# Moving the activation tile H and the coefficient ring by 128 and 256 bytes in a two-block transformer kernel

## The chip, the cores and the metric

The kernel runs on one core of one Trainium2 chip. The metric is the device time of one execution in microseconds (us). A core has five engines with a program each: TensorE (PE, matrix products), VectorE (DVE), ScalarE (ACT), GpSimd (POOL) and SyncE (SP, which here only issues transfers). They share an on-chip memory of 128 partitions, and each tile named below is a range of bytes that is the same in all partitions.

## The reference

Two transformer blocks run one after the other over 256 tokens of width 1024, in float32. What matters of it:

```
# first block
hn = modulate(rmsnorm(x, norm1_g), shift1, scale1);  proj = hn @ w_in
ya = dsa_attention(...);  yb = stick_breaking_attention(...)
x  = x + gate1 * ((sigmoid(ga)*(ya @ w_proj_a) + sigmoid(gb)*(yb @ w_proj_b)) @ w_out)
hn2 = modulate(rmsnorm(x, norm2_g), shift2, scale2)
# expert layer: 16384 experts, 8 heads, 16 experts for each head and token
pre  = einsum('cd,chkd->chk', hn2, u[experts]);  coef = gates * gelu(pre)
x  = x + gate2 * einsum('chk,chkd->cd', coef, v[experts])
# second block
x = x + hybrid_mixer(rmsnorm(x));  x = x + memory_cross_attention(rmsnorm(x), rmsnorm(mem))
h = rmsnorm(x);  u = causal_dwconv(h @ w_up);  x = x + (silu(a) * g) @ w_down
```

The output is a last rmsnorm of x, (1, 256, 1024).

## The kernel before, in words

**Weights as a stream.** All weights come from main memory in units of 128 x 1024 float32 (512 KB). Each unit is split into two float32r parts whose sum is the weight: ACT copies the upper part (line 1298), and DVE (line 1834) or POOL (line 2625) subtracts it from the weight to get the rest. The parts lie in a ring of buffers, `split` (three buffers, lines 377 and 484), with further ones in `split1`, `split4` and `split5` in some phases. Activations are held split in the same way.

**Products.** A product of two split numbers takes three matmuls (`mm3`, line 613, all recorded at line 611): upper x upper, upper x rest, rest x upper. In most layers (`lin`, line 655) the weight is the stationary operand, 128 x 128, and the activations of all 256 tokens are the moving operand, 128 x 256: in the profile `bank<-H,split ... 128x256`. One unit is 24 such matmuls. `bank` is the accumulation memory that TensorE writes.

**The tile H.** `H_all` (line 381) has 16 + 16*256 float32 in each partition. Two views lie in it. `H` (line 382) holds the normed activations, z = 0 the upper parts of eight 128-channel blocks k, z = 1 the rests: each (z, k) is 256 floats, 1024 bytes. It is the moving operand of the input projections, the output projection w_o, the routing projection w_pq, all of `u` and, in the second block, the mixer's and feed-forward's first layer. `Hf` (line 472) is the same memory, 16 floats further on, cut into eight pairs `cf[i]` of 512 floats (line 473): the ring of coefficients of the expert layer's second half.

**The expert layer.** In the u phase PE multiplies all 16384 rows of u with H (128 units, `lin("u", ...)`, line 1023). From unit 56 on, 12 small bf16 matmuls stand between units (`spread_gates`, line 1000), which spread the chosen gates over the experts; their operands lie in turn in `rT` and in the two halves of `xT`. In the v phase (lines 1030 to 1040) the coefficients `cf[i]` are stationary and a v unit is moving, 128 x 512: `bank<-split,H ... 128x512`, 12 a unit. ACT writes the upper part of `cf[i]` (line 1637) and DVE the rest (line 2373), four units ahead.

**The hand-over.** The first coefficients are written over parts of H that PE still reads for the last u unit. So in that unit PE counts up the semaphore `h_past` after k = 2, 4 and 6 (line 693), and ACT waits for it before cf[0], cf[1] and cf[2] (line 1642); cf[3] waits for the end of the unit. cf[0] covers floats 16 to 527 of the tile, and so H's upper parts k = 0, 1 and the first 16 floats of k = 2.

**Where tiles lie.** Tiles get addresses in the order in which they are asked for. Ahead of H stand `ringb` (16384 bytes a partition), `split` (24576), `xT` (8192) and `mod` (48 floats, 192 bytes); behind it `cst`, `vecs`, `sm`, `cond`, `rT`. From `split`'s first byte, `H` begins 24576 + 8192 + 192 = 32960 bytes on, which is 128*256 + 192 (64 bytes short of a multiple of 256), and `Hf` 33024 bytes on, which is 129*256. The tiles `Ya`, `Yb`, `Ym`, `MH` and `act_t`, moving operands as H is, begin 64 bytes short of a multiple of 256 from `split` too, some of them by tiles `gap0` to `gap4` of 64 bytes that hold nothing, and all weight buffers begin at a multiple of 256 bytes from each other.

Of the kernel before, what the change touches and what calls it, by code (L numbers as in the profile page):

```python
# [16 lines left out]
T = 256  # L17
# [56 lines left out]
def flat(ap):  # L74
    return ap.rearrange("p a b -> p (a b)")
# [244 lines left out]
def scaled_before(q):  # L320

    return q - (q > 4)
# [38 lines left out]
def build(nc, A, out, scratch, x_kept):  # L361
    with ExitStack() as ctx:
# [6 lines left out]
        def sb(name, shape, dt=F32, where=ctx):  # L369
            return where.enter_context(nc.sbuf_tensor(name, shape, dt))  # L370
# [5 lines left out]
        ringb = sb("ringb", [128, 4, UNIT])  # L376
        split = sb("split", [128, 3, 2, UNIT], F32R)
        xT = sb("xT", [128, 8, T])
        mod = sb("mod", [128, 48])

        H_all = sb("H", [128, 16 + 16 * T], F32R)
        H = H_all[:, 0:16 * T].rearrange("p (z k t) -> p z k t", z=2, k=8)
        cst = sb("cst", [128, 768])
        vecs = sb("vecs", [128, A["vecs"].shape[1]])
        sm = sb("sm", [128, 160])
        cond = sb("cond", [128, 8])
        rT = sb("rT", [128, 5, T])
# [81 lines left out]
        iota2 = rt[:, 2, 0:128].bitcast(BF16).rearrange("p (i b) -> p i b", b=2)  # L469
        g2 = PR[:, 80 * 256:80 * 256 + 256].rearrange("p (t n) -> p t n", t=2)  # L470
        cpf = PR[:, 81 * 256:81 * 256 + 512].rearrange("p (t z n) -> p t z n", t=2, z=2)
        Hf = H_all[:, 16:16 + 16 * T]
        cf = [(Hf[:, i * 512:i * 512 + 256], Hf[:, i * 512 + 256:i * 512 + 512]) for i in range(8)]

        xkT, xv, bmm, mqT, mkT, mv, ccT, uT, ctmp, gqk, goT, gv, lrT, sc_b, gt = pieces(
# [74 lines left out]
        def evac(name, p):  # L550

            eng, n = EV[name, p]
            return (ev_a if eng == "A" else ev_v, n)
# [13 lines left out]
        def unscaled(q):  # L567

            return (Ym, H, MH)[q - 3], 8 * (q - 3)

# [34 lines left out]
        def tensor_program(t):  # L605
# [7 lines left out]
            def mm3(o, l, r, start, stop):  # L613
                mm(o, l[0], r[0], start, False)
                mm(o, l[0], r[1], False, False)
                return mm(o, l[1], r[0], False, stop)

            def claim(b):
                if freed[b]:
                    t.wait_ge(*freed[b])  # L620
                return banks[b]
# [20 lines left out]
            def unit(name, conc=3):  # L642
                while U[st["pos"]][0] == "w_ada":
                    ada_unit()
                n = st["pos"]
                assert U[n][0] == name, (U[n], name)
                st["pos"] += 1
                jobs.step(conc)
                if P.lo_pool[n]:
                    t.wait_ge(lo_g, P.lo_no[n])  # L650
                else:
                    t.wait_ge(lo_v, P.lo_no[n])
                return buf(n)

            def lin(name, ncols, rhs, need, kt=8, conc=3, after_block=None, after_unit=None, both=False, order=range(8), alone=0, begin=0):
                left = n = 0
                for p in range(begin, ncols // 2):
                    b = None
                    if both and p == begin:


                        b = bank_of[name, p]
                        two = {}
                        steps = [(k, j) for j in range(2) for k in order[:alone]] + [(k, j) for k in order[alone:] for j in range(2)]
                        for k, j in steps:
                            if j not in two:
                                two[j] = unit(name, conc)
                                claim(b)
                            need(k)
                            wh, wl = two[j]  # L670
                            last = mm3(banks[b][:, j * T:(j + 1) * T], (wh[:, k * 128:(k + 1) * 128], wl[:, k * 128:(k + 1) * 128]), rhs(k),
                                       k == order[0] and j == 0, k == order[-1])
                            if k == order[-1]:
                                last.then_inc(pe_done, 1)
                        freed[b] = evac(name, p) if name != "w_up" else (f_t2, 2 * p + 2)
                        if after_block:
                            after_block(p)
                        continue
                    for j in range(2):
                        for k in range(kt):  # L680
                            if left == 0:
                                wh, wl = unit(name, conc)
                                left = 8
                            if b is None:
                                b = bank_of[name, p]
                                claim(b)
                            o = (8 - left) * 128
                            left -= 1
                            need(k)
                            last = mm3(banks[b][:, j * T:(j + 1) * T], (wh[:, o:o + 128], wl[:, o:o + 128]), rhs(k), k == 0, k == kt - 1)  # L690
                            if left == 0 or (j == 1 and k == kt - 1):
                                last.then_inc(pe_done, 1)
                            elif name == "u" and n == 127 and k in (2, 4, 6):

                                last.then_inc(h_past, 1)
                            if left == 0 and after_unit:
                                after_unit(n)
                                n += 1
                    freed[b] = (f_t2, 2 * p + 2) if name == "w_up" else evac("gated" if ("gated", p) in EV and name == "u" else name, p)
                    if after_block:  # L700
                        after_block(p)
# [28 lines left out]
            def of(X):  # L730
                return lambda k: (X[:, 0, k, :], X[:, 1, k, :])

            def of_t(X):
                return lambda k, tt: (X[:, 0, k, tt * 128:(tt + 1) * 128], X[:, 1, k, tt * 128:(tt + 1) * 128])

            hk, hkt = of(H), of_t(H)

# [130 lines left out]

            mh = normed(0)
            lin("w_qi", 4, hk, mh, both=True)  # L870
            one("w_ki", hk, mh)

# [27 lines left out]

            jobs.start(index_steps())
            lin("w_qb", 4, hk, mh)
            lin("w_kb", 4, hk, mh)
            lin_nat("w_vb", hkt, mh, 512)

# [379 lines left out]
        def scalar_program(s):  # L1285
# [68 lines left out]
            def squares(q, name):  # L1354
                def later(c):
                    for i in (2 * c, 2 * c + 1):
                        s.wait_ge(ev_v, EV[name, c][1] - 1 + i % 2)
                        if q in (3, 4):
                            high(q, i)
                    for i in (2 * c, 2 * c + 1):  # L1360
                        square(q, i, xT[:, i, :])
                    yield
                return lambda c: jobs.start(later(c))
# [16 lines left out]
            def hi_of(i):  # L1380
                return MH[:, 0, :, :] if i == 2 else H[:, 0, :, :]

# [171 lines left out]
            for c in range(4):  # L1554
                unit("w_pa")
                s.wait_ge(mg_sum, c + 1)
                S.copy(flat(H[:, 0, 2 * c:2 * c + 2, :]), sg[:, c * 512:(c + 1) * 512]).then_inc(mg_hi, 1)
            add = squares(1, "w_o")
# [265 lines left out]
        def vector_program(v):  # L1824
# [90 lines left out]
            def norm_steps(i, src, gain, shift=None):  # L1915
                for j in range(8 if shift is None else 10):
# [5 lines left out]
                    if shift is not None and j >= 2:  # L1922
                        v.wait_ge(n_hi, 8 * scaled_before(i) + j - 1)
                        V.scalar_tensor_tensor(out=H[:, 1, j - 2, :], in0=rT[:, ROW[(j - 2) % 4], :], scalar=shift(j - 2),
                                               in1=H[:, 0, j - 2, :].bitcast(F32), op0=ALU.add, op1=ALU.subtract).then_inc(n_lo, 1)
# [1016 lines left out]
```

## Time and profile before

| | |
|---|---|
| three runs | 1439.8, 1435.71, 1439.47 us; median 1439.47 |
| profiled execution | 1439.8 us; its span, first to last instruction, 1438.1 us |
| mean granted TensorE clock | 0.988 of full speed |
| PE busy | 1390.4 us, 97% of the span |
| DVE, ACT, POOL busy | 1095.1, 836.4, 359.6 us |
| matmuls | 10406 in the records |

The profile's records give the start and duration of each instruction. A matmul's duration holds its way through the array, and successive matmuls overlap: how fast they follow each other is read from a stretch's length over its count, not from the duration. Some matmul records are missing.

### The profile page before, as it was taken

How to read it: one execution, taken by the hardware profiler on the slowest of the kernel's cores; microseconds unless marked ns; L12 is line 12 of the kernel's file. 1: busy time of each engine (PE TensorE's matmuls, PEld its weight loads, DVE VectorE, ACT ScalarE, POOL GpSimd, SP SyncE). 2: the span in 40 equal slices, each digit the busy share in tenths (PEclk: the TensorE clock that was granted, in tenths of full speed). 3: DMA queues.
4: the chain of work that ended last, by engine and by line, in shares of the span. 5: the costliest groups of instructions: out<-in, count | busy, mean ns of one | idle time of the engine just before them, and what ended most of it. 6: DMA issues, size and time to landing. Idle time of an engine off the chain costs nothing.

```text
span 1438.1 us, 25879 instructions
## 1 busy us (share of the span) xinstructions
PE 1390.4 (97%) x10406; PEld 1292.4 (90%) x10406; DVE 1095.1 (76%) x1903; ACT 836.4 (58%) x1447; POOL 359.6 (25%) x227
## 2 busy tenths in 40 slices
PE   7999999899999999999999999999999999899997
PEld 5988899899999999999988888887889899799997
DVE  7788897567889888999766666677667667798862
ACT  4554774444454687777654454565446666776651
POOL 3216201234445100000032322344322321433200
PEclk9999999999999999999999999999999999999999
DMA  9768775556665454444566666665667636276630
GB/s 387 273 200 266 250 247 170 164 156 184 189 185 161 153 156 148 147 148 147 151 189 221 195 192 195 212 198 178 197 191 254 195 115 193 75 248 191 196 113 30
DMA packets 73721, 268.24 MB, mean 187 GB/s; under 512 B 8401, under 2 KB 9730, under 8 KB 72834
## 3 DMA queue, kind: packets, MB, share of 16 engines
q1 hardware_dynamic: 71280, 256.41, 56.1%
q10 hardware_dynamic: 1426, 7.56, 1.5%
q0 software_dynamic: 896, 2.62, 0.5%
q8 instruction: 83, 1.36, 0.4%
q14 instruction: 36, 0.29, 0.1%
HBM read 262.88 MB, written 3.67 MB: 185 GB/s over the span
## 4 chain that ended last, share of the span: by engine, by line
PE 80%; DVE 13%; ACT 4%; POOL 1%; DMA 1%; issue 1%; DVEq 0%; ACTq 0%; POOLq 0%
PE bank L611 79%; DVE split L1834 3%; DVE ada_acc L1869 2%; DVE PR L2284 1%; DVE PR L2281 1%; DMA ringb<-in_w_ada 1%; POOL H L2652 1%; ACT split L1298 1%; DVE PR L2289 1%; PE bank L787 0%; DVE rT L1920 0%; POOL split L2625 0%; DVE H L2373 0%; DMA vecs<-in_vecs 0%; DVE PA L2085 0%
## 5 line engine op out<-in xcount | busy, mean ns | idle before, releaser
L611 PE MATMUL bank<-H,split 128*128 128x256 f32 x5928 | 724.8, 283 | 17.9 <-DVE split L1834 6.8
L611 PEld LDWEIGHTS bank<-H,split 128*128 128x128 f32 x5928 | 703.1, 191 | 24.7 <-issue 9.4
L1298 ACT CAST split<-ringb 128x1024 fp32r<-128x1024 f32 x350 | 365.9, 1047 | 284.8 <-PE bank L611 270.4
L2625 POOL TENSOR_TENSOR split<-ringb,split 128x1024 fp32r<-128x1024 f32 x91 | 226.7, 2491 | 665.6 <-ACT split L1298 665.6
L611 PE MATMUL bank<-split,H 128*128 128x512 f32 (+1 forms) x1728 | 390.5, 387 | 1.5 <-POOL split L2625 1.5
L1834 DVE TENSOR_TENSOR split<-ringb,split 128x1024 fp32r<-128x1024 f32 x259 | 326.0, 1262 | 74.9 <-ACT split L1298 74.8
L611 PEld LDWEIGHTS bank<-split,H 128*128 128x128 f32 x1728 | 320.9, 188 | 69.1 <-POOL split L2625 2.5
L2373 DVE TENSOR_TENSOR H<-PR,H 128x256 fp32r<-128x256 f32 x128 | 137.3, 1073 | 106.4 <-ACT H L1637 106.4
L1298 ACT CAST split<-far 128x1024 fp32r<-128x1024 f32 x89 | 93.1, 1048 | 53.4 <-PE bank L611 43.1
L1834 DVE TENSOR_TENSOR split<-far,split 128x1024 fp32r<-128x1024 f32 x77 | 99.7, 1304 | 31.5 <-ACT split L1298 31.3
L1613 ACT ACTIVATE PR<-bank 128x512 f32<-128x512 f32 (+31 forms) x59 | 28.7, 487 | 74.5 <-PE bank L611 74.5
L2639 POOL TENSOR_TENSOR rT<-rT 128x256 f32<-128x256 f32 x25 | 26.7, 1067 | 176.4 <-ACT rT L1347 174.8
L611 PE MATMUL bank<-act_t,split 128*128 128x256 f32 x528 | 60.3, 276 | 0.8 <-DVE act_t L2594 0.8
L611 PEld LDWEIGHTS bank<-act_t,split 128*128 128x128 f32 x528 | 60.0, 188 | 1.0 <-DVE act_t L2594 1.0
L1596 ACT ACTIVATE xT<-cst,rT 128x128 bf16<-128x128 f32 x168 | 55.6, 437 | 0.0
L1637 ACT CAST H<-PR 128x256 fp32r<-128x256 f32 x128 | 51.1, 400 | 0.6 <-PE bank L611 0.6
L2346 DVE TENSOR_TENSOR PR<-bank,PR 128x224 f32<-128x224 f32 (+31 forms) x64 | 33.2, 519 | 21.7 <-PE bank L611 21.1
L2336 DVE TENSOR_TENSOR xT<-rt,cpw 128x512 bf16<-128x512 bf16 x126 | 45.7, 417 | 0.0
L2625 POOL TENSOR_TENSOR split<-far,split 128x1024 fp32r<-128x1024 f32 x12 | 30.4, 2530 | 54.6 <-ACT split L1298 54.6
L611 PE MATMUL bank<-Ym,split 128*128 128x256 f32 x336 | 41.7, 283 | 1.5 <-DVE Ym L1995 1.5
L611 PEld LDWEIGHTS bank<-Ym,split 128*128 128x128 f32 x336 | 40.2, 189 | 2.3 <-DVE split L1834 1.7
L611 PE MATMUL bank<-xT 128*128 128x128 bf16 x504 | 36.2, 219 | 0.0
(298 smaller groups left out, 1264.4 us busy)
## 6 DMA issues: line engine op xcount, KB each, us to landing
ringb<-in_u SPq DMA_DIRECT2D x128, 512.0 KB, 3.8
ringb<-in_v SPq DMA_DIRECT2D x128, 512.0 KB, 4.4
ringb<-in_w_ada SPq DMA_DIRECT2D x28, 512.0 KB, 5.4
far<-in_w_up SPq DMA_DIRECT2D x26, 512.0 KB, 4.3
far<-in_w_ada SPq DMA_DIRECT2D x20, 512.0 KB, 5.2
ringb<-in_w_up SPq DMA_DIRECT2D x17, 512.0 KB, 4.7
ringb<-in_w_pq SPq DMA_DIRECT2D x16, 512.0 KB, 4.2
far<-in_w_dn SPq DMA_DIRECT2D x14, 512.0 KB, 4.2
```

What stands on the lines that cost most here:

```text
L611: return TE.matmul(o, l, r, start=start, stop=stop, skip_group_check=True)
L1298: S.copy(buf(m)[0], slots[P.slot[m]]).then_inc(hi_done, 1)
L1596: S.activation(z[:, i // 2, :, i % 2], iota, ACT.Abs, bias=cpn[:, 4 * g + i:4 * g + i + 1]).then_inc(t_abs, 1)
L1613: ins = S.activation(d[:, :, n:T], o[:, :, n:T], ACT.Gelu)
L1637: S.copy(cf[i % 8][0], P3[:, i, :]).then_inc(c_hi, 1)
L1834: V.tensor_tensor(lo, slots[P.slot[m]], hi.bitcast(F32), ALU.subtract).then_inc(lo_v, 1)
L1869: V.scalar_tensor_tensor(out=acc, in0=w, scalar=cond[:, k:k + 1], in1=acc, op0=ALU.mult, op1=ALU.add).then_inc(ada_done, 1)
L2336: ins = V.tensor_tensor(t_gate[g % 3][:, z, :, :, :], t_col[g % 2], of_four(gp[:, 2 + z, :], g), ALU.mult)
L2346: V.tensor_tensor(d[:, 0:n, :], o[:, 0:n, :], d[:, 0:n, :], ALU.mult).then_inc(t_out, 1)
L2373: V.tensor_tensor(lo, P3[:, i, :], hi.bitcast(F32), ALU.subtract).then_inc(c_lo, 1)
L2625: G.tensor_tensor(lo, slots[P.slot[m]], hi.bitcast(F32), ALU.subtract).then_inc(lo_g, 1)
L2639: G.tensor_tensor(acc, acc if k > 1 else rT[:, square_row(q, 0), :], rT[:, square_row(q, k), :], ALU.add).then_inc(sq_add, 1)
```

## The change

The first edit places `mod` behind `vecs` instead of ahead of H; so H_all, cst and vecs begin 192 bytes lower. The second lets `H` begin at float 16 of H_all (it was float 0) and `Hf` at float 0 (it was float 16). With both, `H` lies 128 bytes lower than before and `Hf` 256 bytes lower. From `split`'s first byte `H` is then at 32832 = 128*256 + 64, and `Hf` at 32768 = 128*256. cst and vecs lie 192 bytes lower, mod behind them; no other tile moves. The third edit fits the hand-over to this: cf[0] now covers floats 0 to 511 and so k = 0 and the larger part of k = 1, and PE counts after k = 1, 3 and 5. On all five engines the same instructions stand in the same order as before.

```diff
         xT = sb("xT", [128, 8, T])
-        mod = sb("mod", [128, 48])
 
         H_all = sb("H", [128, 16 + 16 * T], F32R)
-        H = H_all[:, 0:16 * T].rearrange("p (z k t) -> p z k t", z=2, k=8)
+        H = H_all[:, 16:16 + 16 * T].rearrange("p (z k t) -> p z k t", z=2, k=8)
         cst = sb("cst", [128, 768])
         vecs = sb("vecs", [128, A["vecs"].shape[1]])
+        mod = sb("mod", [128, 48])
         sm = sb("sm", [128, 160])
...
-        Hf = H_all[:, 16:16 + 16 * T]
+        Hf = H_all[:, 0:16 * T]
         cf = [(Hf[:, i * 512:i * 512 + 256], Hf[:, i * 512 + 256:i * 512 + 512]) for i in range(8)]
...
-                            elif name == "u" and n == 127 and k in (2, 4, 6):
+                            elif name == "u" and n == 127 and k in (1, 3, 5):
 
                                 last.then_inc(h_past, 1)
```

## Rows read from the trace of the kernel before

**Rows 1.** The page, part 1: busy time, share of the span, instructions.
```profile
PE 1390.4 (97%) x10406; PEld 1292.4 (90%) x10406; DVE 1095.1 (76%) x1903; ACT 836.4 (58%) x1447; POOL 359.6 (25%) x227
```

**Rows 2.** The chain that ended last: start us, us, what.
```profile
35.86 17.20 PE bank L611 x144
...
315.72 102.91 PE bank L611 x872
...
483.60 249.97 PE bank L611 x2493
...
736.74 238.27 PE bank L611 x1050
...
1257.23 109.11 PE bank L611 x936
```

**Rows 3.** The page, part 5: line, operation, count | busy, mean ns | idle before.
```profile
L611 PE MATMUL bank<-H,split 128*128 128x256 f32 x5928 | 724.8, 283 | 17.9 <-DVE split L1834 6.8
```

**Rows 4.** Windows, all engines: us, busy by engine (count), clock, DMA share, GB/s.
```profile
316.00:419.00 103.00, 103.00 (x877) 103.00 (x876) 84.09 (x292) 50.89 (x59) 42.86 (x18) 1.00 0.61 183
487.00:733.00 246.00, 246.00 (x2460) 243.42 (x2458) 211.95 (x434) 179.15 (x404) 7.19 (x3) 1.00 0.51 153
```

**Rows 5.** Windows, PE alone, matmuls that read or write tile H.
```profile
320.00:400.00 80.00, 80.00 (x682) 1.00 0.61 185
1280.00:1340.00 60.00, 60.00 (x532) 1.00 0.62 195
...
750.00:900.00 150.00, 150.00 (x663) 1.00 0.65 201
1119.00:1126.00 7.00, 7.00 (x32) 1.00 0.82 237
```

**Rows 6.** Tile H on PE, 320 to 400 us: duration min/median/max.
```profile
L611 PE MATMUL bank<-H,split x682: 281/281/281, 319.7 to 400.0; 128*128 128x256 f32 x171
```

**Rows 7.** Tile H on PE, 1280 to 1340 us.
```profile
L611 PE MATMUL bank<-H,split x532: 276/276/276, 1279.8 to 1340.0; 128*128 128x256 f32 x178
```

**Rows 8.** Timeline of PE in the u phase: start us, us, operation, count.
```profile
583.05 3.07 PE L611 MATMUL bank<-H,split 128*128 128x256 f32 x24
585.96 0.86 PE L611 MATMUL bank<-xT 128*128 128x128 bf16 x12
...
590.21 2.99 PE L611 MATMUL bank<-H,split 128*128 128x256 f32 x24
593.04 0.86 PE L611 MATMUL bank<-rT 128*128 128x128 bf16 x12
```

**Rows 9.** Timeline of PE in the w_pq projection, key scores between.
```profile
273.15 5.91 PE L611 MATMUL bank<-H,split 128*128 128x256 f32 x48
278.90 1.05 PE L611 MATMUL bank<-PR 128*128 128x128 f32 x8
279.71 5.71 PE L611 MATMUL bank<-H,split 128*128 128x256 f32 x48
285.25 0.94 PE L611 MATMUL bank<-PR 128*128 128x128 f32 x7
```

**Rows 10.** Tiles Yb and act_t on PE, whole span: duration min/median/max.
```profile
L611 PE MATMUL bank<-Yb,split x96: 276/281/387, 201.9 to 215.1; 128*128 128x256 f32 x96
...
L611 PE MATMUL bank<-act_t,split x528: 276/276/386, 1366.2 to 1427.0; 128*128 128x256 f32 x176
```

**Rows 11.** Matmuls with cst, by line and form.
```profile
L611 PE MATMUL bank<-rT,cst 128*128 128x256 f32 x46 | 14.2, 454 | 1.9 <-ACT rT L1347 1.9
```

**Rows 12.** Timeline of all engines at the hand-over from u to v.
```profile
733.59 0.76 ACT L1637 CAST H<-PR 128x256 fp32r<-128x256 f32 x2 [0.30 <-PE bank L611]
...
733.74 4.43 PE L611 MATMUL bank<-split,H 128*128 128x512 f32 x17
...
734.25 0.58 ACT L1615 ACTIVATE bank<-bank 128x512 f32<-128x512 f32 x1
...
735.48 1.21 DVE L1834 TENSOR_TENSOR split<-ringb,split 128x1024 fp32r<-128x1024 f32 x1
...
736.74 1.23 PEld L611 LDWEIGHTS bank<-split,H 128*128 128x128 f32 x6 [0.49 <-DVE split L1834]
```

## The prediction

> **What bounds the kernel now.** I read the page's busy times first: PE is busy for 1390.4 of 1438.1 us [rows 1]. The chain of waits, in order of time, then says where PE itself sets the end [rows 2]: five long pieces without a wait in them, 17.20 us at 36, 102.91 at 316, 249.97 at 484, 238.27 at 737 and 109.11 at 1257, together 717 us. In the two pieces that matter most the other engines have room: from 316 to 419 us DVE is busy for 84.09 of 103 us, ACT for 50.89, and the DMA engines for 0.61 of the time; from 487 to 733 us it is 211.95 and 179.15 of 246, and 0.51 [rows 4]. PE is without a gap in both. What shortens PE's matmuls there shortens the kernel by as much; what lengthens them does the same.
>
> The instructions and their order do not change, so the question is whether an address changes the speed of an instruction. The reader should look at the same instruction at two places: a 128x256 matmul with H moving and a weight of `split` stationary. From 320 to 400 us 682 records fill 80.00 us, from 1280 to 1340 us 532 fill 60.00 [rows 5]. Taking off the two that only hang over an edge, one starts every 80.00/680 = 117.6 ns in the first and every 60.00/530 = 113.2 ns in the second. The granted clock is 1.00 in both windows, so this is not the clock. The durations say the same without an edge: 281/281/281 ns against 276/276/276 [rows 6, 7]. There are two settled rates, and the difference is 4.4 ns a matmul, nearly 4%. I call them slow and fast.
>
> Over the whole span the mean with H is 283 ns for 5928 matmuls [rows 3], with some at the slower clock in it; by the stretches counted below about 2,900 of them, half, are slow. What selects a rate? Within a stretch it is constant over all k, upper and rest, and over all buffers of the ring: 872 matmuls in 102.91 us from 316 us on, 118.0 ns each, all slow [rows 2]. It changes only where other matmuls stand between. In the w_pq projection, 48 matmuls from 273.15 to the key scores at 278.90 take 5.75 us and the next 48, from 279.71 to 285.25, take 5.54 us [rows 9]; this alternation goes on for eight groups. In the u phase the unit from 583.05 to 585.96 takes 2.91 us, that from 590.21 to 593.04 2.83 us [rows 8], and the pattern slow, slow, fast repeats over the 64 gate groups. Other moving tiles, which lie 64 bytes short of a multiple of 256 bytes from `split` as H does, show both too: Yb has 276 as its smallest and 281 as its median, act_t 276 as its median over 528 [rows 10]. So at this distance both rates are stable once entered. That looks like two streams of reads, moving operand and next weights, that get in each other's way or not, depending on how they stand to each other. Where they stand is what an address distance sets.
>
> **The change, part by part.**
>
> *H against split, from 64 bytes below a multiple of 256 to 64 above.* Nothing in the trace has a 256-wide matmul at the new distance with the weight stationary, so I bound the cost from both sides by the two rates that exist. All H stretches fast, where PE sets the end:
> - 36 to 53 us, 144 slow: 144 x 4.4 ns = 0.64 us.
> - w_pq, four slow groups of 48: 4 x (5.75 - 5.54) = 0.84 us.
> - 316 to 419 us, 872 slow: 3.84 us.
> - u phase: of 64 units with gates 43 slow at 2.91 - 2.83 = 0.08 us, 3.44 us, and eight units after the last gates (711 to 733 us, 186 matmuls) at 24 x 4.4 ns, 0.84 us.
> - the rest (slow parts of the attention projections, the routing stretch 419 to 483 us where DVE sets the pace half of the time, and the second block's short layers): an estimate from some 450 slow matmuls, 2.0 us, of which half counts, 1.0 us.
>
> The sum is 0.64 + 0.84 + 3.84 + 4.28 + 1.0 = 10.6 us of gain. Nothing takes it back as long as DVE has the 19 and 34 us of room of [rows 4]; in the u phase a fast unit already exists every third time without PE waiting.
>
> All H stretches slow: the feed-forward's 936 matmuls from 1257 us on [rows 2] lose 4.1 us, 21 fast u units 1.7, w_pq 0.8, the 165 behind the first piece 0.7, and the other fast ones, some 1100 in the attention and mixer layers, 4.8 us of which 3.7 count since other engines set the pace in part. That is 11.0 us of loss. So this term is between -10.6 and +11.0 us. I take -10.6: half of the matmuls are slow at the old distance, which is therefore no good one, and the other half shows that nothing in the instruction stream forbids the fast rate. It is a choice, not a derivation.
>
> *Coefficients, Hf, 256 bytes lower.* Its distance to `split` stays a multiple of 256. In the v phase 663 records fill 150.00 us [rows 5], 150.00/661 = 226.9 ns, twice the fast rate. The nearest other row has H itself as the stationary operand with a 512-wide moving one, at a distance of 64 bytes: 7.00 us for 32 records [rows 5], or about 30.5 matmuls, 229 ns. So the price of a bad place is 2.3 ns x 1536 = 3.5 us, and there is none better in the trace. I take 0, because the distance modulo 256 is kept, and keep 0 to +3.5 for the range.
>
> *H as the stationary operand* in the value projections: 192 matmuls, 144 of them 512 wide, at most 2.3 ns each, below 0.5 us either way. I take 0.
>
> *cst 192 bytes lower.* It is the ones or identity operand. The largest group is 46 matmuls, 14.2 us [rows 11]; with 4% on these and the few like them, 0.6 us on either side. I take 0. mod and vecs are read by vector instructions of a few hundred nanoseconds, for which no row hints at an effect of the address.
>
> *Hand-over one k earlier.* In the last u unit PE counts `h_past` one group of three matmuls earlier, 0.35 us. PE goes from its last u matmul to its first v matmul without a gap at 733.74 [rows 12], so nothing is won there. The one wait of PE is 0.49 us at 736.74 for the rest part of the second v unit, which DVE starts at 735.48. Queued ahead of it on DVE is the product that waits for ACT's Gelu at 734.25, which needs the end of the u phase. ACT's third and fourth casts are at 733.59; the third can go 0.35 us earlier, the fourth waits for the last u matmul as before, so the Gelu moves by less than 0.1 us. Worth 0 to -0.1 us; I take 0.
>
> **Sum.** -10.6 us on the profiled execution: its span 1438.1 becomes 1427.5, its time 1439.8 becomes 1429.2. The median of the runs, 1439.47, lies 0.3 us below that execution; so 1428.9 us, rounded to 1429.
>
> **A rule against it.** The rows above show one instruction at two rates at one clock, and the 4.4 ns between them. The Trainium skill says otherwise on both counts. "SBUF — State Buffer", section "Who interferes with whom", gives TensorE one read port for the moving operand and an independent one for the weights, and states that "PE and ACT never wait on anyone"; "TensorE: Matmul & The Clock Gate", section "Wait — 56ns, not 53.3ns?", gives the warm start-to-start as N / 2.4 GHz plus about 2.5 ns, 109.2 ns for N = 256, with no word of an address. By these the change would do nothing and the time would be 1439.5 us. The trace does not agree with them in size, 113.2 and 117.6 ns; whether the address is what they miss, no row shows.
>
> **The rivals.**
>
> *No net effect.* The rate may be picked by how TensorE comes out of the small matmuls and waits between units, which the change leaves as they are; or both rates stay stable at the new distance and the stretches are dealt anew. For it: both rates occur at one and the same distance, and groups of 48 alternate while their addresses repeat. Against it: in the value projections and the v phase two distances give 229 and 226.9 ns for one shape [rows 5], with no 226.9 in the one and no 229 in the other. If nothing changes, 1439.5 us. If they are dealt anew in the same proportion, the two long blocks, 3.8 us at 316 and 4.1 us at 1257, may go either way: 1435 to 1443.
>
> *The slow rate everywhere.* At the new distance each matmul with H meets the weight reads. The place is the feed-forward's first layer at 1257 to 1366 us, now wholly fast, then 117.6 instead of 113.2 ns. For it: all tiles of the kernel's fastest stretches (act_t, H in the feed-forward) have the old distance and none the new; where H was stationary and the distance was 64 bytes the other way, the 512-wide rate was the worse. Against it: the old distance is slow half of the time as well. It decides from the point at which more than half of the H matmuls are slow; in full, +11.0 us, 1450.5 us.
>
> *The coefficients pay.* H gets fast but the v phase gets the 229 ns: 1429 + 3.5 = 1432.5; with H unchanged, 1443.
>
> **How the numbers follow.** Forecast (H mostly fast) 0.42, own range 1426 to 1434. No net effect 0.27. Slow rate 0.27. Coefficients or something outside the two rates 0.04. What a measurement of this kernel can tell from no change is about 0.3%, 4.3 us. Faster holds the forecast, a part of the deal-anew case and half of the last, 0.45; slower the slow case and a part of the deal-anew case, 0.30; within 0.3% the remaining 0.25. The range goes from 1425 to 1451: the lower end is the full gain with some of the mixed stretches counted whole, the upper end the full loss.
>
> **What would show it.** Right: in the window 320 to 400 us the median duration with H is 276 ns and the count rises to about 708; the chain's piece of 872 matmuls takes 99 us; all u units between gates take 2.83 us; the v phase keeps 226.9 ns; act_t and Yb keep theirs. Wrong: a median of 281 in the feed-forward, or the same alternation as in [rows 8, 9] at the same places (then the address has no part), or a third rate, which would be outside my bounds.

## The result, and the profile after

The changed kernel takes 1447.41 us, the median of 10 runs (1441.86 to 1453.23), the kernel before, run beside it, 1436.3 us (1433.6 to 1439.8): a ratio of 1.0068, with an interval from 1.0046 to 1.0091. The ratio is worked out over 15 executions of the changed kernel, with a median of 1446.3 us; by it the change costs 10 us, by the two medians above 11. The forecast was 1429 us and faster; the range up to 1451 holds the result, but the forecast went to the wrong side. It was the rival "the slow rate everywhere" that happened, priced at 1450.5 us.

The profiled execution of the changed kernel has a span of 1450.8 us, 12.7 us above before; the mean granted clock is 0.988 in both. Its busy times, beside [rows 1]:

```profile
PE 1402.9 (97%) x10406; PEld 1303.3 (90%) x10406; DVE 1097.6 (76%) x1903; ACT 836.6 (58%) x1447; POOL 358.2 (25%) x227
```

PE is busy for 12.5 us more with the same 10406 matmuls; the other engines are as they were. The chain that ended last, in order of time, has the same pieces as [rows 2]; the first shown here holds w_pq (start us, us, what):

```profile
265.87 54.34 PE bank L611 x440
320.96 102.90 PE bank L611 x872
...
488.85 252.44 PE bank L611 x2496
...
744.11 238.31 PE bank L611 x1050
...
1267.05 112.06 PE bank L611 x936
```

The piece of 872, all slow before, is unchanged to 0.01 us. The u phase is 2.5 us longer, the v phase the same, the feed-forward 2.95 us longer. The starts tell where the rest is lost: 5.2 us by the piece that began at 483.60 and now begins at 488.85, 7.4 us at the v phase, 9.8 us at the feed-forward.

Not all of this is the change. A second profile of the kernel before (the last experiment) has a span of 1439.9 us, 1.8 us more than the first, and reaches the last four of these pieces at 317.75, 485.96, 739.17 and 1260.27 us. Against it the changed kernel is 3.2, 2.9, 4.9 and 6.8 us late there and 10.9 us longer in all, which agrees with the medians. The length of the feed-forward piece also depends on the clock at its start. By tile H, the first 10 us of the piece before, after, and in the second profile of before (us, busy, count, clock, DMA share, GB/s):

```profile
1257.00:1267.00 10.00, 9.77 (x62) 0.70 0.88 304
...
1267.00:1277.00 10.00, 9.95 (x71) 0.83 0.88 308
...
1260.00:1270.00 10.00, 9.73 (x71) 0.83 0.86 306
```

The granted clock there was 0.70 in the first profile of before and 0.83 in the other two. At the same 0.83 the piece takes 108.00 us before and 112.06 after, 4.06 us more and not 2.95.

The windows of the matmuls with H, in each case moved along with their stretch, beside [rows 5] (us, busy, count, clock, DMA share, GB/s):

```profile
325.00:405.00 80.00, 80.00 (x682) 1.00 0.59 185
1285.00:1345.00 60.00, 60.00 (x511) 1.00 0.61 191
760.00:910.00 150.00, 150.00 (x664) 1.00 0.63 200
```

In the feed-forward 511 records fill 60 us where 532 did. With two off for the edges this is 117.9 ns a matmul in place of 113.2, at a granted clock of 1.00 both times. The durations in that window, beside [rows 7]:

```profile
L611 PE MATMUL bank<-H,split x511: 279/279/280, 1284.8 to 1344.9; 128*128 128x256 f32 x171
```

They are 279 ns, not the 281 of the slow stretches before [rows 6]; the pace is the same, though, 117.9 beside 117.6 ns. It pays to read the pace from count and length, and not the duration alone. The timeline of PE in the u phase, beside [rows 8], and in the w_pq projection, beside [rows 9]:

```profile
585.71 3.07 PE L611 MATMUL bank<-H,split 128*128 128x256 f32 x24
588.62 0.86 PE L611 MATMUL bank<-rT 128*128 128x128 bf16 x12
589.29 3.07 PE L611 MATMUL bank<-H,split 128*128 128x256 f32 x24
592.21 0.86 PE L611 MATMUL bank<-xT 128*128 128x128 bf16 x12
592.88 3.07 PE L611 MATMUL bank<-H,split 128*128 128x256 f32 x24
...
277.84 5.90 PE L611 MATMUL bank<-H,split 128*128 128x256 f32 x48
283.58 1.05 PE L611 MATMUL bank<-PR 128*128 128x128 f32 x8
284.39 5.90 PE L611 MATMUL bank<-H,split 128*128 128x256 f32 x48
290.13 1.05 PE L611 MATMUL bank<-PR 128*128 128x128 f32 x8
```

The pattern slow, slow, fast is gone, each unit takes 2.91 us, and so is the alternation: 5.74 us for every group of 48. act_t, which did not move, keeps its median of 276 ns:

```profile
L611 PE MATMUL bank<-act_t,split x528: 276/276/386, 1378.9 to 1439.7; 128*128 128x256 f32 x176
```

### The profile page after: what moved, and what is told of

It reads as the page before. It is cut to its first block, busy times and chain, and to the rows that moved or that the text cites. A ratio compares the mean times of both kernels' runs of the same rounds, so it can differ in the third digit from the quotient of the medians.

```text
span 1450.8 us, 25879 instructions
## 1 busy us (share of the span) xinstructions
PE 1402.9 (97%) x10406; PEld 1303.3 (90%) x10406; DVE 1097.6 (76%) x1903; ACT 836.6 (58%) x1447; POOL 358.2 (25%) x227
## 4 chain that ended last, share of the span: by engine, by line
PE 80%; DVE 13%; ACT 4%; DMA 1%; POOL 1%; issue 1%; DVEq 0%; ACTq 0%; POOLq 0%
PE bank L611 79%; DVE split L1834 3%; DVE ada_acc L1869 2%; DVE PR L2284 1%; DVE PR L2281 1%; ACT split L1298 1%; DMA ringb<-in_w_ada 1%; DVE PR L2289 1%; POOL H L2652 0%; DVE rT L1920 0%; PE bank L787 0%; POOL split L2625 0%; DMA vecs<-in_vecs 0%; DVE H L2373 0%; DVE PA L2085 0%
## 5 line engine op out<-in xcount | busy, mean ns | idle before, releaser
L611 PE MATMUL bank<-H,split 128*128 128x256 f32 x5928 | 736.3, 283 | 17.1 <-DVE split L1834 7.1
L611 PEld LDWEIGHTS bank<-H,split 128*128 128x128 f32 x5928 | 713.8, 190 | 24.1 <-DVE split L1834 9.4
```

Of the source, the lines that this page charges most:

```text
L611: return TE.matmul(o, l, r, start=start, stop=stop, skip_group_check=True)
```

## The experiments

The theory at this point (D): the distance from the weights in `split` to H, modulo 256 bytes, decides which rates exist, 64 below a multiple both, 64 above the slow one alone. Against it stood C (the moved coefficients or small tiles cost the time) and E (stretches are dealt anew by how TensorE enters them, the address has no part). In all runs but H alone and the kernel before once more, `mod` is written over the bias it is made from, with this edit, which makes room for the tiles that move. The edits below are excerpts:

```diff
-        mod = sb("mod", [128, 48])
+        mod = vecs[:, VO["b_ada"]:VO["b_ada"] + 48]
```

**H alone.**

```diff
-        H_all = sb("H", [128, 16 + 16 * T], F32R)
-        H = H_all[:, 0:16 * T]
+        H_all = sb("H", [128, 32 + 16 * T], F32R)
+        H = H_all[:, 32:32 + 16 * T]
-        sm = sb("sm", [128, 160])
+        sm = sb("sm", [128, 144])
-        k in (2, 4, 6)
+        k in (1, 3, 5)
```

> Only H moves: its view begins 128 bytes higher (distance from split 64 above a multiple of 256 in place of 64 below); the coefficients stay at the address of before, mod stays ahead of H, cst and vecs go 64 bytes up. PE's hand-over count is after k = 1, 3, 5. Theory D (the distance of H from the weights, modulo 256 bytes, decides): nearly all 128x256 matmuls with H at 281 ns, u units between gates 2.91 us each, the stretch behind 1257 us slow, and the time that of the change, 1.005 to 1.009 of before, about +10 us. Rival E (the stretches are dealt anew by how TensorE enters them, and the address has no part of its own): the u phase keeps slow, slow, fast or gets another mixture, and the time is within 4 us of before. Rival C (the moved coefficients or the new places of cst, vecs and mod cost the time): H at 276 and 281 in equal parts as before, and the time of before.

Measured: 1447.47 us against 1436.32, ratio 1.0077 (1.0052 to 1.0103). The whole loss is there with the coefficients and mod in their old places and cst and vecs only 64 bytes from theirs. In the chain the u piece takes 252.34 us and the feed-forward 113.10.

**Coefficients alone.** H at float 48 of a tile that begins 192 bytes lower is at its old address.

```diff
+        H_all = sb("H", [128, 64 + 16 * T], F32R)
+        H = H_all[:, 48:48 + 16 * T]
+        Hf = H_all[:, 0:16 * T]
-        k in (2, 4, 6)
+        k in (1, 3, 5)
```

> H stays at its address of before; the coefficients go 256 bytes down as in the change, with the hand-over count after k = 1, 3, 5; mod gives up its tile and is written over the bias b_ada in vecs, so that cst, vecs and all later tiles keep their addresses. Theory D: H matmuls as before (half at 276, half at 281 ns, u phase slow, slow, fast, feed-forward fast), v phase 226.9 ns a matmul, time within 3 us of before. Rival C: the +10 us of the change come here too. Rival E: the stretches are dealt in another way than before although no address of H or split moved.

Measured: 1434.99 us, ratio 0.9988 (0.9967 to 1.0009), so no loss beyond 0.1%: the coefficients are cleared, and with them the hand-over, which is that of the change here. cst and vecs have not moved in this run; they are cleared by the run with H alone, which has the whole loss without their 192 bytes. So C falls. One piece is not as in the first profile:

```profile
316.65 99.08 PE bank L612 x872
```

All 872 are fast, with H and split at their old addresses. The u phase is slow, slow, fast as before (250.40 us). The forecast of D, "as before", missed the 872; E has its share in the truth.

**split moved, H not.** 32 floats of nothing ahead of split; H stays at its absolute address and is then 64 above. xT moves with split; sm is made 64 bytes longer than before, so that rT stays.

```diff
+        sb("gap_x", [128, 32])
         split = sb("split", [128, 3, 2, UNIT], F32R)
```

> H stays at its absolute address of before, and the weight buffers of split go 128 bytes up, so that the distance from split to H is 64 above a multiple of 256, as in the change; cf stays at a multiple of 256 from split. The buffers split1, split4 and split5 keep their addresses, so that H is 64 below them as before. mod is written over b_ada. Theory D in its relative form (only the distance counts): the w_pq projection and the u phase, which use split alone, are wholly slow (281 ns, u units 2.91 us, 872 matmuls from 316 us on in about 102.9 us), while layers that use the other buffers too are mixed; time +4 to +10 us. Absolute form (H's own address counts): u phase slow, slow, fast as before, time within 3 us of before.

Measured: 1440.63 us, ratio 1.0023 (1.0000 to 1.0047). In the chain and, for 1280 to 1340 us, by tile H:

```profile
317.61 102.91 PE bank L613 x872
...
485.49 252.45 PE bank L613 x2496
...
1263.32 106.59 PE bank L613 x936
...
L613 PE MATMUL bank<-H,split x532: 276/276/276, 1279.7 to 1339.9; 128*128 128x256 f32 x178
```

The u phase, where all weights come from split, is as slow as in the change (252.45), although H has not moved: H's own address does not decide. The feed-forward, where four of seven weight buffers are still 64 above H, is fast throughout, also for the three that are not. Its piece is shorter than before because the clock was 1.00 from its start. The price in time, 4 us by the medians, is at the lower edge of the +4 to +10 expected. In the chain it shows where split alone is used: the piece with w_pq in it takes 54.30 us (52.89 before), the u piece 2.5 us more.

**Both moved.** The same gap ahead of ringb, H at float 48; split and H each 128 bytes up, the old distance.

> split and H both go 128 bytes up, so that their distance is the old one, 64 below a multiple of 256; cf is at a multiple of 256 from split; split1, split4 and split5 stay, and H is 64 above a multiple of 256 from them. mod is written over b_ada. Relative form of theory D: w_pq and u phase (split alone) as before, slow, slow, fast with 2.91, 2.91, 2.83 us a unit; layers that use the other buffers too (feed-forward) may become slow, up to +4 us; time 0 to +4 us. Absolute form: everything with H slow as in the change, +10 us.

Measured: 1434.46 us, ratio 0.999 (0.9969 to 1.0011): no loss with both moved. So neither H's address nor split's decides, but the distance: one of them moved alone costs time in the u phase, both together do not. The feed-forward is fast too (912 matmuls in 103.66 us), although H is here 64 above four of its seven buffers; the loss of up to 4 us that was thought possible did not come. The u phase, though, is faster than before, 246.06 us in place of 249.97:

```profile
483.99 246.06 PE bank L613 x2496
```

All units between gates are fast here, which no theory had foretold.

**Other distances.** The layout of the run with the coefficients alone, with H at float 0, 32, 40 and 56 in place of 48:

```diff
-        H = H_all[:, 48:48 + 16 * T]
+        H = H_all[:, 0:16 * T]
```

> H begins at a multiple of 256 bytes from split (float 0 of its tile, 65664), everything else as in the run with only the coefficients moved. Theory D, graded: the slow rate comes from the weight read meeting the H read, and a distance of 64 above is where they meet and stay together. If the meeting spreads 64 bytes to both sides, 0 is slow as well, time +10 us or more; if the distances act as a sharp value, 0 is fast or mixed, -11 to 0 us. Rival (only 64-byte oddness counts, as both 64 below and 64 above have it): 0 has a third rate, below 276 or above 281 ns.

> H begins 128 bytes above a multiple of 256 from split. If the price falls with the distance from 64 above on both sides alike, this is as 0 is. If it grows from 64 below (half slow) over 0 to 64 above (all slow) and falls again, 128 is between and mixed. Fast throughout would be 276 ns for all H matmuls, u units 2.83 us, and a time 10 to 12 us below before.

> H begins 160 bytes above a multiple of 256 from split (96 below the next), between 128 and the old distance of 192. Theory D with a smooth price: at least as good as before, 0 to -11 us, with more than half of the H matmuls at 276 ns. With a price by 64-byte steps alone: not aligned to 64 bytes, the moving read touches one line more, all matmuls slower than 281 ns, and the time above before.

> H begins 224 bytes above a multiple of 256 from split (32 below the next), between the old distance and 0. The same two answers as at 160: smooth price, mixed or fast, 0 to -11 us; price by 64-byte steps, all slower.

| H above split, modulo 256 | time, us | ratio to before, interval | 872 matmuls, us | feed-forward, us |
|---|---|---|---|---|
| 0 | 1455.76 | 1.0102, 1.0070 to 1.0134 | 104.81 | 114.07 |
| 64 (H alone) | 1447.47 | 1.0077, 1.0052 to 1.0103 | 102.91 | 113.10 |
| 128 | 1453.44 | 1.0091, 1.0058 to 1.0123 | 103.68 | 112.88 |
| 160 | 1450.30 | 1.0090, 1.0056 to 1.0124 | 103.68 | 111.35 |
| 192 (coefficients alone) | 1434.99 | 0.9988, 0.9967 to 1.0009 | 99.08 | 107.86 |
| 224 | 1452.85 | 1.0096, 1.0069 to 1.0122 | 103.38 | 112.56 |

The rows 64 and 192 were measured beside a before of 1436.32 us, the other four beside one of 1438.52, with four to nine executions each; the ratios are what to compare. No other distance tried is as good as the old one, and the price is not smooth: 32 bytes to either side cost what the change costs. The guess that it falls off evenly around 64 is wrong. The rival of 64-byte steps is not borne out either: 0 and 128 are multiples of 64, and cost as much as 160 and 224, which are not. The lengths of the feed-forward pieces hold the clock at their start as well (1.00 in the run at 160, lower in the others) and tell the distances apart less surely than the 872 do, which ran at 1.00. By this count a slow matmul takes 102.91/872 = 118.0 ns and a fast one 99.08/872 = 113.6. At 0 there is a third rate, 104.81/872 = 120.2 ns:

```profile
L612 PE MATMUL bank<-H,split x585: 283/283/283, 329.8 to 399.9; 128*128 128x256 f32 x195
```

At 128 the durations spread from 279 to 285 ns in the same window. So the slow rate was no upper bound either; a third rate above 281 ns at 0 is what one of the rivals had.

**What stands between.** Why were all u units fast when split and H were shifted together? One thing that shift did: rT, the operand of every third gate group, came to a multiple of 256 from split, as xT had been all along. Theory G: the matmuls in between select the rate, by their own distance. H at its old address, rT 128 bytes lower:

```diff
-        sm = sb("sm", [128, 160])
+        sm = sb("sm", [128, 144])
         rT = sb("rT", [128, 5, T])
+        sb("gap_r", [128, 32])
```

with `H_all` of 48 + 16 * T floats. cst, vecs and sm go 64 bytes down by this and cond 128, as rT does.

> H at its address of before (64 below a multiple of 256 from split). Changed: rT, from which every third group of gate matmuls reads, goes 128 bytes down, so that it is at a multiple of 256 from split, as the other two groups' operand xT is already; in the run in which split was shifted by 128 bytes the same held, and there all u units between gates were fast. cst and vecs go 64 bytes down, mod is written over b_ada. Theory G (what stands between the H matmuls throws TensorE into the slow rate if it lies at an odd place to split): all 64 units between gates at 276 ns and 2.83 us, u phase 3.4 us shorter, time 1429 to 1433. Rival E (chance or time of entry): slow, slow, fast or another mixture, time as before.

Measured: 1434.07 us against 1439.11, ratio 0.9968 (0.9949 to 0.9988). The chain's piece and the timeline of PE:

```profile
482.78 246.06 PE bank L613 x2496
```

```profile
587.13 0.86 PE L613 MATMUL bank<-xT 128*128 128x128 bf16 x12
587.80 2.99 PE L613 MATMUL bank<-H,split 128*128 128x256 f32 x24
590.63 0.86 PE L613 MATMUL bank<-rT 128*128 128x128 bf16 x12
591.30 2.99 PE L613 MATMUL bank<-H,split 128*128 128x256 f32 x24
```

All units between gates take 2.83 us, and the piece is 3.9 us shorter than in [rows 2]; 3.4 had been foretold. `mod` written over the bias is not the reason: the run with the coefficients alone had that too, and its units were slow, slow, fast. By the ratio the kernel is 0.3% faster than the kernel before; the time, 1434.07 us beside a before of 1439.11, is just above the 1429 to 1433 expected.

**The key scores too.** As above, and

```diff
-        qh = [PR[:, 22528 + i * 512:22528 + (i + 1) * 512] for i in range(3)]
-        skt = PR[:, 80 * 256:80 * 256 + 2048]
+        qh = [PR[:, 22560 + i * 512:22560 + (i + 1) * 512] for i in range(3)]
+        skt = PR[:, 80 * 256 + 32:80 * 256 + 2080]
```

> As the run with rT moved, and the key scores' operands qh and the sub-keys go 128 bytes up, to a multiple of 256 from split. Theory G: the alternation of the w_pq projection ends too, all eight groups of 48 at 5.54 us, and the stretch of 872 matmuls behind them is fast, 98.9 us; time 8 to 10 us below before. Rival E: w_pq alternates or is dealt anew, no more than 4 us.

Measured: 1433.01 us against 1439.11, ratio 0.9966 (0.9944 to 0.9989), no different from the run above and short of the 8 to 10 us expected. The alternation in w_pq is still there:

```profile
273.07 5.90 PE L613 MATMUL bank<-H,split 128*128 128x256 f32 x48
278.81 1.06 PE L613 MATMUL bank<-PR 128*128 128x128 f32 x8
279.62 5.70 PE L613 MATMUL bank<-H,split 128*128 128x256 f32 x48
285.16 1.05 PE L613 MATMUL bank<-PR 128*128 128x128 f32 x8
```

So G does not hold for every kind of matmul in between. The 872 matmuls were fast in this profile (99.08 us), but so they were in the run with the coefficients alone, where the key scores had not moved; that part is not put down to the edit.

**rT moved, H 64 above.**

> As the run with rT moved, but H 64 above a multiple of 256 from split, as in the change. Theory D: the slow rate everywhere, u units 2.91 us whatever stands between, time that of the change, +10 us. If G alone decided and not the distance of H: u units fast, time at or below before.

Measured: 1450.7 us, ratio 1.0075 (1.0057 to 1.0094); u piece 252.34 us, feed-forward 112.06. At the distance of the change the rT move does not bring the fast rate back. The run with split moved and H not had said as much: there too rT was at a multiple of 256 from split, and the u phase was slow.

**The kernel before once more.**

> The kernel before, word for word, for a second profile. If the rates were fixed by the program alone, w_pq alternates, the 872 matmuls behind it take 102.9 us (slow), the u units are slow, slow, fast and the feed-forward is fast, all as in the first profile. If a stretch is dealt anew in every execution, at least one of these differs, and this is what spreads the times of before over 1429 to 1446 us.

Measured: 1441.75 us, one run. The u units are slow, slow, fast (250.04 us for the piece), the 872 slow (102.91), the feed-forward fast. But another piece of the chain, 53.28 us in, 20.36 us long and fast in the first profile, is now slow:

```profile
54.48 21.09 PE bank L611 x184
...
264.20 52.80 PE bank L611 x440
317.75 102.91 PE bank L611 x872
...
485.96 250.04 PE bank L611 x2493
...
1260.27 108.00 PE bank L611 x936
```

The granted clock was 1.00 over the H matmuls of this piece, from 56 to 72 us, in both profiles; 144 of them started there before, with a median of 276 ns, and 139 here, with 281.

One program, word for word, has some stretches at one rate in one execution and at the other in the next, while others came out alike in both profiles. That this is what spreads the times of one program is not shown: of the 15 executions of the changed kernel the two with the lowest mean granted clock, 0.986, were the slowest, 1453.11 and 1453.23 us, and the one with the highest, 0.993, took 1443.21, so the clock has a part in it.

## Why the prediction was wrong, point by point

**What bounds the kernel, and the two rates: right.** PE's pace is what moved, by 12.5 us of busy time in a span 12.7 us longer. Both rates returned in later profiles, 117.9 ns for the feed-forward after the change and 276 ns for act_t beside it. The five pieces of [rows 2] were not all in which PE sets the end; the chain also has 52.89 us at 262 and 91.82 at 996, for example.

**The step that failed: "I take -10.6".** The term for H against split was bounded from -10.6 to +11.0 us, and the value chosen was the wrong end. Measured it is +10 to +11 us: 1447.41 against 1436.3, and 1447.47 against 1436.32 with H alone, what the slow case had in full. The reason given was that half of the matmuls were slow at the old distance, "which is therefore no good one". The runs show that the old distance is the only one of six tried at which the fast rate is found in the u phase and in the 872 matmuls ahead of it. Half slow was not a sign of a bad place: at the old distance a stretch can be at either rate, and in the change, with H 64 above all weight buffers, the stretches looked at were at the slow one alone. The rows held a warning: every moving tile of the kernel had the same distance, the fastest stretches among them, and no row had a fast 256-wide matmul elsewhere. That was listed under the slow rival and weighed 0.27.

**The price of 4.4 ns: right for this change, wrong as a bound.** With the second profile of before as the measure, the feed-forward lost 4.06 us (4.1 in the slow case), the u piece 2.4 (1.7), and the piece with w_pq in it, 54.34 us after 52.80, 1.5 (0.8); the 872, slow already, lost nothing. What the other layers lost is the rest of 10.9 us, 2.9 (4.4). At a distance of 0, though, the same matmul takes 120.2 ns. The sign of being wrong, a median of 281 ns in the feed-forward, did not come as written: the median is 279, and it is the pace of 117.9 ns that shows the slow rate.

**Coefficients: right.** 0 was taken; the v piece is 238.31 us after 238.27, and the run with them alone is within 0.3% of before.

**H as the stationary operand: too small to matter, but not 0.** Of the 144 wide matmuls the first 48, at 75.48 us, took 11.11 us until the next group began, 231 ns each; after the change, at 77.64 us, they took 11.30, 235 ns. That is 4 ns each, not the 2.3 allowed, and 0.6 us if all 144 pay it. The rate is dealt here too: the 48 of the second block took 11.08 us before, 11.30 after, and 11.29 in the second profile of before. The 229 ns of the prediction came from 32 records in 7 us, too few to tell 229 from 231.

**cst, vecs, mod: right** as far as the runs tell. cst and vecs moved by 64 bytes in the runs with both moved and with rT moved, without a loss. Their 192 bytes were in the change alone, which lost no more than H alone.

**Hand-over: right.** Nothing that can be told, by the run with the coefficients alone; after the change the wait of PE for the second v unit is 0.51 us, 0.49 before [rows 12].

**The rule against it.** The statement of the Trainium skill in "SBUF — State Buffer", section "Who interferes with whom", that PE waits on no one was read as a case for no effect. No run tests it between engines, but a matmul's pace here depends on where its two operands lie to each other: moving split and leaving H slowed the u piece from 249.97 to 252.45 us. Whether it is the two reads that collide, as the prediction supposed, was not shown; no run takes one of the reads away.

**The rival "no net effect"** had a true part: the rate of a stretch can be dealt anew, as the second profile of before shows. It works within what the distance allows.

What stays open: why 32 bytes either way spoil it, why w_pq alternates, and why the feed-forward stays fast when only some of its weight buffers have the good distance. That the rT move acts through its distance from split, rather than by something else in its address, rests on two layouts (rT moved, and split with H moved; the run with the key scores repeats the first), in both of which all u units between gates were fast. In both, cst, vecs and sm also lay 64 bytes and cond 128 bytes closer to split than before, and no run parts these from rT; of them PE reads none from 484 to 733 us.

## What to carry to other kernels

Where a stretch has TensorE without gaps, look at whether the same matmul has two paces in one profile at one clock. If it has, the placing of stationary and moving operand to each other is worth a scan of a few offsets, measured, one tile at a time; a place with a mixed pace may be the best one, and the way in, the matmuls in between, may be what to mend. Several profiles of one kernel are needed, since a stretch can change its rate from one to the next. Nothing here lets one work out the good offset beforehand.

## What the runs showed of the hardware

- For 128x256 float32r matmuls at a granted clock of 1.00, pace by H's distance from split modulo 256 bytes, from the piece of 872: 113.6 or 118.0 ns at 192, 118.0 at 64, 118.6 at 224, 118.9 at 128 and 160, 120.2 at 0.
- In the profiles of the two kernels the slow matmuls last 281 ns at 192 and 279 at 64, at the same pace.
- A rate once entered outlives changes of buffer: 872 matmuls in a row, and a feed-forward that stays fast with three (split moved) or four (both moved) of its seven weight buffers at the bad distance.
- A tile that did not move can change its rate between runs; whether what runs ahead of it or the execution does this is not shown. Ya, at 276 or 277 in eleven profiles, was slow in those with H at 0, 128 and 160. At 0:

```profile
L612 PE MATMUL bank<-Ya,split x96: 281/281/281, 215.3 to 226.4; 128*128 128x256 f32 x96
```
